# Gate products of a hybrid mixer layer as seven block products for eight, with sums on GpSimd and VectorE

## The reference

```python
ga, gb, gc = jnp.split(jax.nn.sigmoid(h @ w_gate_l + b_gate_l), N_BRANCH, axis=-1)
y = (ga * (oa @ w_br_l[0]) + gb * (ob @ w_br_l[1]) + gc * (oc @ w_br_l[2])) @ w_o_l
```

## Time and profile before

| | us |
|---|---|
| median of 3 runs | 2165.5 (2165.38 to 2169.61) |
| span of the profiled execution | 2168.7 |
| PE busy | 2054.0 |
| DVE busy | 1131.9 |
| ACT busy | 508.2 |
| POOL busy | 196.2 |

### The profile page before, as it was taken

The page is one execution under the profiler, slowest core; times in us unless marked ns, Lnnn a source line. Parts: engine busy times, 40 slices in busy tenths (PEclk is TensorE's granted clock), DMA queues, the critical chain, the costliest instruction groups (busy, mean ns, idle before and its releaser), DMA issues. The chain is left out here.

```text
span 2168.7 us, 25186 instructions
## 1 busy us (share of the span) xinstructions
PE 2054.0 (95%) x9738; PEld 1212.0 (56%) x9738; DVE 1131.9 (52%) x1782; ACT 508.2 (23%) x1007; POOL 196.2 (9%) x234
## 2 busy tenths in 40 slices
PE   7999999999999999699899999999999999969996
PEld 3457766576467654344244676656755676434432
DVE  1135458343447765756342453764534444866664
ACT  2014300242134400122130342003412342002221
POOL 1000010020110000100120002001101000010003
PEclk9999999999999999899999999999999999989997
DMA  7311146411122161689771112562111114238996
GB/s 303 129 47 39 37 144 237 138 54 44 39 81 98 68 278 75 252 342 359 265 256 39 63 35 69 199 214 86 47 53 49 42 40 172 91 136 313 382 350 186
DMA packets 62681, 317.01 MB, mean 146 GB/s; under 512 B 14824, under 2 KB 15280, under 8 KB 34272
## 3 DMA queue, kind: packets, MB, share of 16 engines
q1 hardware_dynamic: 32688, 232.41, 28.6%
q0 software_dynamic: 13136, 53.64, 7.6%
q10 hardware_dynamic: 16736, 29.32, 3.8%
HBM read 286.70 MB, written 27.07 MB: 145 GB/s over the span
## 5 line engine op out<-in xcount | busy, mean ns | idle before, releaser
L1081 PE MATMUL ps<-hT,ring 128*128 128x320 f32 x2048 | 604.0, 438 | 0.0
L1081 PEld LDWEIGHTS ps<-hT,ring 128*128 128x128 f32 x2048 | 369.7, 190 | 138.3 <-issue 3.3
L1081 PE MATMUL ps<-ring,hT 128*128 128x512 f32 (+1 forms) x960 | 386.6, 558 | 2.5 <-DVE hT L1995 1.7
L1081 PE MATMUL ps<-ring,zT 128*128 128x512 f32 (+2 forms) x992 | 317.6, 600 | 2.0 <-ACT zT L1898 2.0
L1081 PEld LDWEIGHTS ps<-ring,hT 128*128 128x128 f32 x960 | 178.8, 190 | 184.0 <-issue 174.8
L1081 PE MATMUL ps<-R,ring 128*128 128x512 f32 (+1 forms) x768 | 211.1, 435 | 4.6 <-DVE zT L2267 3.2
L1081 PEld LDWEIGHTS ps<-ring,zT 128*128 128x128 f32 (+2 forms) x992 | 121.5, 156 | 149.1 <-issue 146.3
L1830 ACT COPY R<-ps 128x512 f32<-128x512 f32 (+2 forms) x170 | 96.1, 565 | 374.7 <-PE ps L1330 372.5
L1081 PEld LDWEIGHTS ps<-R,ring 128*128 128x128 f32 x768 | 116.9, 191 | 99.3 <-issue 93.1
L2112 DVE SCALAR_TENSOR_TENSOR R<-ring,cs,R 128x2048 f32<-128x2048 f32 x56 | 131.7, 2352 | 5.5 <-DMA ring<-in_wall 3.5
L2193 DVE RECIPROCAL rinv<-rsum 128x2 f32<-128x2 f32 x96 | 15.9, 166 | 224.6 <-ACT R L1816 224.6
(11 more groups left out here) (302 smaller groups left out, 2045.7 us busy)
## 6 DMA issues: line engine op xcount, KB each, us to landing
ring<-in_wall SPq DMA_DIRECT2D x188, 1024.0 KB, 6.1
hT<-in_wall SPq DMA_DIRECT2D x20, 1024.0 KB, 8.5
y_all<-R ACTq DMA_DIRECT2D x27, 512.0 KB, 7.0
R<-in_wall SPq DMA_DIRECT2D x10, 1024.0 KB, 9.2
R<-in_rows POOLq DMA_DIRECT2D x2, 4096.0 KB, 15.7
R<-mrows POOLq DMA_DIRECT2D x16, 512.0 KB, 19.2
R<-in_x ACTq DMA_DIRECT2D x10, 512.0 KB, 9.5
h_rows<-R ACTq DMA_DIRECT2D x10, 512.0 KB, 2.6
```

Source lines behind the costliest of these rows:

```text
L1081: ins = nc.tensor.matmul(out, w, m, start=start, stop=stop, **kw)
```

## The change

A pair of tiles m, both halves of the channels and both halves of the tokens form a 2 x 2 by 2 x 2 block product. It is computed as seven products of four steps (k blocks) instead of eight, by sums of weight blocks and of token blocks. 28 steps make a pair, 112 a branch.

- GpSimd forms the sums of tokens (`token_sum`, 4 x 320 columns each) once for A and once for B and C, and four sums of weights a pair (`first_sums`: three, after the sixth product of the pair before; `last_sum`: one, after the second product), 4 x 128 columns each. In C's projection the first sums stand ahead of the powers for chunk 7.
- VectorE adds the products from PSUM into `sg` (`add_products`, six additions of 320 columns a pair), after the maximum of an item and after its normalisation.
- ScalarE copies the first product (LOW_LOW), and takes three tanh a pair: two of 320 columns, one of 640. In `attend` all of it now stands ahead of `keep_probs`.
- TensorE: a product waits for the product two before it in the same bank to be read, and for its sums. The "after" steps go from 3 to 2 in B, from 3 or 2 to 2 or 1 in A, and in C from 3 to 1, with "between" from 3 to 4; C's second tail fill goes from 8 to 4 and item 0's "between" from 4 to 8.
- From the gates of B on, single use pieces go through four ring slots; two (`KEPT_SLOTS`) hold sums of tokens until C's gates are done.

The core of the diff, deep indentation cut by twelve:

```diff
 SLOT_COUNT = ITEMS + 1
-TAIL_FILL = (8, 0, 8)
+TAIL_FILL = ((8,), (), (8, 4))
 UNIT_FILL = 2
 FILL = (
-    ((0, 6, 0),) + 6 * ((0, 4, 3),) + 4 * ((0, 4, 2),) + 6 * ((0, 4, 3),) + ((0, 6, 0),),
-    ((4, 6, 0),) + 16 * ((0, 4, 3),) + ((0, 6, 0),),
-    ((0, 4, 0),) + 16 * ((0, 3, 3),) + ((0, 4, 0),),
+    ((0, 6, 0),) + 12 * ((0, 4, 2),) + 4 * ((0, 4, 1),) + ((0, 6, 0),),
+    ((4, 6, 0),) + 16 * ((0, 4, 2),) + ((0, 6, 0),),
+    ((0, 8, 0),) + 16 * ((0, 4, 1),) + ((0, 4, 0),),
 )
+PAIRS = 4
+STEPS = 4
+SEVEN = 7
+LOW_LOW, CROSS, HIGH_LOW, DOWN, ACROSS, LATE, HIGH_HIGH = range(SEVEN)
+ADDS = 6
+SUMS = 4
+SIGMOIDS = 3
 PIECE = 2048
...
 FIRST_B = [p.index((layer, ("in", CHUNKS[1][0], 0))) for layer, p in enumerate(STREAM)]
-SKIPPED = len(PROJECT_SLOTS) - 2
 MOE_FIRST = [p.index((layer, MOE_LOADS[0])) for layer, p in enumerate(STREAM)]
 ALL_SLOTS = SLOTS + 3
+KEPT_SLOTS = (4, 5)
+TURNS = (2, 3, 0, 1)
+def narrow_pieces(layer):
+    return MOE_FIRST[layer] - 4 - FIRST_B[layer] - len(PROJECT_SLOTS)
+def place_in_ring(layer, i):
+    j = i - FIRST_B[layer]
+    if j < 0:
+        return i % SLOTS
+    n = narrow_pieces(layer)
+    w = j - len(PROJECT_SLOTS)
+    if w < 0:
+        at = PROJECT_SLOTS[j]
+    elif w < n:
+        at = TURNS[w % 4]
+    else:
+        at = (*KEPT_SLOTS, TURNS[n % 4], TURNS[(n + 1) % 4], TURNS[(n + 2) % 4], TURNS[(n + 3) % 4])[w - n]
+    return (FIRST_B[layer] + at) % SLOTS
 def moe_slots(ring):
...
-n = [TAIL_FILL[br] * LAST_QK[br] + (UNIT_FILL * LAT if br == 2 else 0)]
+n = [sum(TAIL_FILL[br]) + (UNIT_FILL * LAT if br == 2 else 0)]
 for before, between, after in FILL[br]:
     n += [before, between, after]
-assert sum(n) == 16 * KB, (br, sum(n))
+assert sum(n) == PAIRS * SEVEN * STEPS, (br, sum(n))
 return n
-        def halves(br, s, at):
-n = fills(br)
-done = sum(n[:1 + 3 * s + at])
...
+        def gate_no(br, p, o):
+return SEVEN * (PAIRS * br + p) + o + 1
+        def adds_by(br, p, o):
+return ADDS * (PAIRS * br + p) + (0, 1, 1, 2, 4, 5, 6)[o]
+        def quarters(br, p):
+m = 2 * p
+return (sg[br][:, m, 0:320], sg[br][:, m, 320:640], sg[br][:, m + 1, 0:320], sg[br][:, m + 1, 320:640])
...
             lay, what = pieces[i]
+            if what == ("o", 0, 0):
+                sp.wait_ge(pe_gate, gate_no(2, PAIRS - 1, HIGH_HIGH))
...
+                ch.step(nc.gpsimd.tensor_tensor(dst, a, b, ALU.subtract), g_tok)
+        def gate_piece(br, p):
+            i = pieces.index((layer, ("gate", br, p)))
+            return i, slot_at(slot_of(layer, i)).rearrange("p (k n) -> p k n", k=8)
+        def first_sums(br, p):
...
+            pool.wait_ge(full[slot_of(layer, i)], 16 * loads_by(layer, i))
+            if br or p:
+                pool.wait_ge(pe_gate, gate_no(br, p, LOW_LOW) - SEVEN + LATE)
+            ch.step(nc.gpsimd.tensor_tensor(part_sum, w[:, low, 128:256], w[:, high, 128:256], ALU.add), g_sum)
+            ch.step(nc.gpsimd.tensor_tensor(cross_sum[:], part_sum, w[:, low, 0:128], ALU.subtract), g_sum)
+            ch.step(nc.gpsimd.tensor_tensor(w[:, low, 128:256], w[:, low, 0:128], w[:, low, 128:256], ALU.subtract), g_sum)
...
+            i, w = gate_piece(br, p)
+            pool.wait_ge(pe_gate, gate_no(br, p, CROSS))
...
+        summed = [[0, 0] for _ in range(3)]
+        def gate_sums(br, n):
...
+                    if SEVEN * b + CROSS + 1 > n:
+                        return
+                    last_sum(br, b)
+                    summed[br][1] += 1
+                else:
+                    if a == PAIRS or (a and SEVEN * (a - 1) + LATE + 1 > n):
+                        return
+                    first_sums(br, a)
+                    summed[br][0] += 1
...
+                token_sum(2, 3)
             for c in CHUNKS[br]:
+                if c == 7:
+                    gate_sums(2, 0)
                 if c in (6, 7):
                     for t in range(NT):
                         pool.wait_ge(v_sq, 5 + 5 * (c - 6) + t + 1)
...
+                    for j in range(4):
+                        token_sum(1, j)
+                    pool.wait_ge(mrow_out, 16 * 2 * STRIPS)
+                    gate_sums(1, 0)
                 i = PU.index((br, c, CTX))
                 typ = CHUNK_TYPE[c]
                 if typ == "k" and turned(c):
...
-                    pool.wait_ge(v_sq, u + 1)
+                if c == 2:
+                    pool.wait_ge(a_hT, KB // 2 * NT if layer else KB)
+                    pool.wait_ge(v_hT, KB // 2 * NT if layer else KB)
+                    if layer:
+                        pool.wait_ge(x_out, 16)
+                    for j in range(4):
+                        token_sum(0, j)
+                    gate_sums(0, 0)
+            for s in range(ITEMS + 2):
+                if s:
+                    gate_sums(br, products_by(br, min(s, SLOT_COUNT) - 1, 2))
+                if br == 0 and s >= 2 and unit_done(s - 2) is not None:
+                    pool.wait_ge(v_sq, unit_done(s - 2) + 1)
                     powers(small[:, 8:12], small[:, 0:4])
-            if br == 1:
...
-                    if b < 3:
+                if br == 1 and 1 <= s <= 12:
+                    b, g = lat(s + 4)
+                    masked_bias(b, g)
+                    if g == LAT - 1 and b < 3:
                         load_bias(b + 1)
         pool.wait_ge(pe_pv, 3 * ITEMS)
...
             for _ in range(n):
-                h, k = divmod(filled[0] - 16 * KB * br, KB)
-                m, part = divmod(h, 2)
-                if k == 0:
-                    if h < 2:
-                        if n_mod[0]:
+                p, step = divmod(filled[0] - PAIRS * SEVEN * STEPS * br, SEVEN * STEPS)
+                o, k = divmod(step, STEPS)
+                w = take("gate", ahead).rearrange("p (k n) -> p k n", k=8)
+                if o == LOW_LOW:
+                    if k == 0:
+                        if br or p:
+                            pe.wait_ge(v_part, adds_by(br, p, LOW_LOW) - 1)
+                        if p == 0 and n_mod[0]:
                             pe.wait_ge(a_mod, n_mod[0])
...
-                    else:
-                        pe.wait_ge(a_sg, 16 * br + h - 1)
-                w = take("gate", ahead).rearrange("p (k n) -> p k n", k=8)
-                ins = mm(ps[:, 6 + part, 0:320], w[:, k, 128 * (m % 2):128 * (m % 2) + 128], hT[:, k, 320 * part:320 * part + 320],
-                         k == 0, k == KB - 1, frees=k < KB - 1)
-                if k == KB - 1:
+                    weights, tokens = w[:, k, 0:128], hT[:, k, 0:320]
+                elif o == CROSS:
+                    if k == 0:
+                        if br or p:
+                            pe.wait_ge(v_part, adds_by(br, p, LOW_LOW))
+                        pe.wait_ge(g_sum, SUMS * (PAIRS * br + p) + 2)
+                        pe.wait_ge(g_tok, sums_ready(br, 1))
+                    weights, tokens = cross_sum[:, k, :], token_row(layer, br, 1, k)
+                elif o == HIGH_LOW:
+                    if k == 0:
+                        pe.wait_ge(a_low, PAIRS * br + p + 1)
+                    weights, tokens = w[:, 4 + k, 0:128], hT[:, 4 + k, 0:320]
+                elif o == DOWN:
+                    if k == 0:
+                        pe.wait_ge(v_part, adds_by(br, p, CROSS))
+                        pe.wait_ge(g_sum, SUMS * (PAIRS * br + p) + 3)
+                        pe.wait_ge(g_tok, sums_ready(br, 2))
+                    weights, tokens = w[:, k, 128:256], token_row(layer, br, 2, k)
+                elif o == ACROSS:
+                    if k == 0:
+                        pe.wait_ge(a_sg, SIGMOIDS * (PAIRS * br + p) + 1)
+                        pe.wait_ge(g_tok, sums_ready(br, 0))
+                    weights, tokens = part_sum[:, k, :], token_row(layer, br, 0, k)
+                elif o == LATE:
+                    if k == 0:
+                        pe.wait_ge(v_part, adds_by(br, p, DOWN))
+                        pe.wait_ge(g_sum, SUMS * (PAIRS * br + p) + 4)
+                    weights, tokens = cross_sum[:, k, :], hT[:, 4 + k, 320:640]
+                else:
+                    if k == 0:
+                        pe.wait_ge(v_part, adds_by(br, p, ACROSS))
+                        pe.wait_ge(g_tok, sums_ready(br, 3))
+                    weights, tokens = w[:, 4 + k, 128:256], token_row(layer, br, 3, k)
+                ins = mm(ps[:, 6 + (SEVEN * p + o) % 2, 0:320], weights, tokens, k == 0 and o != HIGH_LOW, k == STEPS - 1,
+                         frees=k < STEPS - 1, skip_group_check=o in (LOW_LOW, HIGH_LOW))
+                if k == STEPS - 1:
                     ins.then_inc(pe_gate, 1)
-                    if h % 4 == 3:
+                    if o == HIGH_HIGH:
                         used(1)
                 filled[0] += 1
...
+        def sigmoids(br, n_direct, n_added):
+            done = PAIRS * SEVEN * br
+            def sigmoid(dst, src, m):
```

(56 more changed lines are left out.)

120 lines of the change are left out of this document (82 added, 38 removed).

## The result

The changed kernel takes 2183.81 us (median of 4 runs, 2181.7 to 2187.68), the kernel before on the same chip 2167.28 us (4 runs, 2165.38 to 2169.61): the ratio is 1.0075, with a 95% interval of 1.0061 to 1.0089. It is slower by 0.75%, where the forecast was 0.2% faster, and 2183.81 lies outside the range of 2149 to 2175.

The account below looks back on a forecast made before the run. PE was taken as the bound, busy 95% of the span, with the exponentials' path limiting what removed steps save. Products -12.8 us and sums +9.3 gave -3.5: 2165.5 to 2162.0 us, range 2149 to 2175 for 8 in 10.

Parts of the forecast that it names:

- the start of C: C's item 0: steps moved in from the tail fill waits, a product waits for a late addition; cancels to +0.2 us.
- The step and the items: Branch loops: a gate step takes 0.537 us; changed items take 6.77 us in A, 5.74 in B, 7.17 in C.
- The steps pay in full: Rival for the branch loops: the exponentials' path moves with the steps, 51.6 us less, 2114 to 2123; chance 0.03.
- GpSimd's sums: Sums of 1.45 us delay VectorE's two-operand SBUF instructions at five places a layer; +9.3 us, bounds 0 and 14.5.
- long sums: Rival at the same ten places: a GpSimd sum takes 2.2 us instead of 1.45; +9.2 us in total, 2174.7; chance 0.15.
- two thirds: Share of the 14.5 us bound taken for VectorE waiting beside GpSimd's sums, since the second waits only for the rest; 9.3 us.
- upper bound of 14.5: VectorE beside GpSimd: at ten places an instruction on the path waits for one whole sum of 1.45 us; 14.5 us.
- the ScalarE case: At A's item 8, B's item 4, C's item 1, queued tanhs delay the copies of probabilities; 0.7 to 0.8 us each.
- The start of B: Before B's first transpositions the fourth product waits for an addition behind item 0's normalisation; addition and two steps, 1.6 us.
- VectorE's additions cost nothing but the two places: 24 additions of 0.49 us a stage are covered by waits for exponentials, except at two named places.
- Transfers at 0: Ring with four single-use slots instead of six from B's gates on: cost 0; 1 to 2 us once if late.
- -12.8: Sum of the products over both layers, in us: A -2.7 and B -6.1 a layer, C +1.8 and +3.0.

Follow-up runs that it names:

- e1: Kernel before without the last two of 16 gate products a branch, no sums or additions, steps taken from behind the transpositions; 2248.3 us, total not comparable with before.
- e2: As e1, the same work left out, but in A and C the steps are taken from between scores and transpositions; 2224.4 us, total not comparable with before.
- e15: e8 with A's additions before norm_output, norm_output one item later, the next layer's accumulation between maximum and reciprocal, B's output copies before the maximum; 2131.34 us, ratio 0.9823.
- e16: e15 with the gate steps of A and C taken from behind the transpositions, as in the changed kernel; 2152.2 us, ratio 0.9928.
- e5: Changed kernel with four gate steps of C's item 0 moved back into the tail; 2177.3 us, ratio 1.0037.
- e7: Changed kernel with VectorE's additions in item 0 of each branch put ahead of that item's normalisation; 2172.94 us, ratio 1.0013.
- e6: Changed kernel with ScalarE's tanhs that wait for VectorE's additions put behind the item's exponentials; 2177.23 us, ratio 1.0032.
- e11: e8 with the finished output of B and C copied out of PSUM ahead of the item's maximum; 2154.75 us, ratio 0.9925.
- e3: Changed kernel with every GpSimd weight sum cut from 128 to 4 columns a block; 2168.91 us, ratio 1.0000 to the kernel before.
- e4: Changed kernel with one step of each item of A and C moved from ahead of the transpositions to behind them; 2171.75 us, ratio 1.0025.
- e12: e8 with A's additions ahead of norm_output and the output copies of B and C ahead of the maximum; 2144.52 us, ratio 0.9891.
- e8: Changed kernel with the edits of e5, e6 and e7, steps as in e4, and C's first three sums spread singly behind three powers; 2156.28 us, ratio 0.9937.

## Why the prediction was wrong, step by step

The forecast for the median was -3.5 us; measured were +16.5. The largest single error is the start of C, which was called even; the clock behind waits, which has no term, runs through three of the items below.

- **The step and the items: right.** 0.537 us a step, items of 6.77, 5.74 and 7.17 us, the small waits before A's scores. "The steps pay in full" fell, as it was given 0.03. That a step behind the transpositions is worth little and one ahead its whole is shown by e1 and e2, and by e15 and e16.
- **GpSimd's sums: the right mechanism, under-sized.** 14.9 us instead of 9.3. The places were the right ones (C's projection, A's first output). A sum is 1.26 us rather than 1.45, so "long sums" falls. Two steps failed. Beside a sum the products were held 0.94 to 1.09 us, three quarters or more of a sum rather than two thirds, and where PE waits already all of it goes to PE: its wait in C's projection grew by 2.03 us in each layer. And behind that wait the clock fell, for which the forecast has no term: the two stretches grew by 8.4 us, 4.3 more than the two waits. That the total lies near the upper bound of 14.5 is luck, since ten sums of 1.26 us would be 12.6 and the bound holds no clock.
- **The start of C: the step that failed.** "Steps moved from the tail into item 0 fill waits ... that cancels to +0.2." The addition's place was seen and called even. From C's first scores to its third the changed kernel takes 5.6 + 13.56 = 19.2 us in layer 0 and 18.4 in layer 1, before it took 12.3; less 2.15 for the four steps that no longer stand in the tail, 4.7 and 3.9 us are lost, where the forecast had 1.0 a layer (0.2, the ScalarE case of 0.7 and an item longer by 0.12). PE waits 2.64 us for the addition, and the clock takes up to 3.0 more. e5 undoes the queue place: 6.5 us.
- **The start of B: right, but for the clock.** The queue place was named and priced at 1.6 us, two steps and an addition. Without additions the item takes 7.23 us (e1). In layer 1 it takes 8.95, 1.7 more; in layer 0, with PE's steps at half the clock behind the same wait of 2.49 us, 10.33, 3.1 more. e7, which mends it together with C's start, gives 10.9 us.
- **ScalarE's case: right mechanism, half the size.** 0.7 to 0.8 us a time were forecast, 1.38 came. The estimate of 0.8 for a tanh of 640 columns was right (0.83); what it left out is the tanh of the sixth product, 0.56 us, which stands ahead of it in the same item. Mending all gives 6.6 us (e6) instead of 2 x (0.7 + 0.8 + 0.7) = 4.4.
- **The clock: put at nothing.** The forecast has no term for it. In windows of 2 us the kernel before keeps a granted clock of 1.00 in all of its branch stages. The changed kernel has five stretches at 0.50: at the start of B in layer 0, and in C's projection and at C's start in both layers. Each window's missing share of the clock, times its length, adds up to 11.9 us. In part of it PE still waits, so this is an upper estimate of what the slow clock cost, of the 20.0 us between forecast and measurement. It is contained in the terms above and not to be added to them.
- **Not seen at all:** the output copies of B, behind two additions (items 2 and 10 each 0.8 us longer, 3.2 in all). "VectorE's additions cost nothing but the two places" was too narrow: e11 shows that they cost where a copy out of PSUM stands behind them. In C of layer 0 three items grew by 0.8 to 1.2 us, where one was foreseen.
- **Transfers at 0: right.** None of PE's waits in the loops was ended by one.

The terms add up roughly: -12.8 + 14.9 (sums) + 6.6 (C's start, beyond 1.0 a layer) + 1.6 (B's, beyond 1.6 a layer) + 2.2 (ScalarE, beyond 4.4) + 3.2 (B's copies) = +15.7. The last four come from the profiled loops and from e6 and partly overlap with each other and with the sums (without the sums C's item is 12.12 us rather than 13.56, without the tanh 11.58), so that this shows the size and is no proof of each.

What stays open: why the clock falls behind a wait in one layer or kernel and not in another. It moves single stages of the profiled executions by 1 to 2 us (the start of B, C of layer 0), so that differences of this size between two profiles are not to be read as an effect of an edit. And e15 still has an item of 8.7 us in layer 0's C: two scalings (L2443) take 2.71 us instead of 1.14 beside sums. That later sums would mend it wasn't tried.

## What to carry to other kernels

Work taken from a bound engine is worth what its consumers' path lets through: find for each place which chain releases the next step, and take the work from ahead of that point. Every small instruction that the change adds to another engine has a place in an in-order queue; ask what PE waits for behind it at the first items of a loop, where nothing covers, and at the rare items (a finished output, a copy out of PSUM). The same products were worth +0.75% or -1.8% by such places (a few of the moves concern work that was there before). Price interference at nearly the whole of the other engine's instruction where the bound engine waits already, and add what the clock may take behind the longer wait.

## What was not expected of the hardware

- **The clock after a short wait.** In the branch stages, where PE otherwise hardly waits, the granted clock fell to 0.50 (1.2 GHz) for some us behind single waits: 2.64 us (four steps then took 4.60 us instead of 2.42), 3.37 and 3.82 (16 projection matmuls took 5.31 and 4.60 instead of 3.62). A wait of 2.64 us so cost 5.6 and 4.3. But the same wait did not always do it. Behind 2.49 us at the start of B the clock fell in 4 of 10 cases (two layers of the changed kernel, e3, e4, e5 and e6), behind 1.75 us in layer 0's C in e12 and not in e11. It stayed up behind the 1.79 us of the kernel before in both layers.
- **Interference is recorded as work.** VectorE's instructions get longer (a product 0.69 to between 1.41 and 1.78 us, an accumulation 2.35 to 3.06, two scalings of one SBUF input each 1.14 to 2.71). GpSimd's do too: a sum goes from 1.26 to 1.60 beside a product, and to 3.20 in e8, where it began 0.99 us after that accumulation. No idle time appears, so a view of waits doesn't show it; a group's mean against the one before does. The maximum of A and C, which reads PSUM alone, stayed at 1.49 us in all 64 cases.
